# Seven products for one more k pair, and a new order of VectorE's work, in the down stages of a fused fp32 block

## What is computed

```
z = rmsnorm(h, norm2_w) @ mlp_w1          # 2048 -> 8192
h = h + jnp.square(jax.nn.relu(z)) @ mlp_w2   # 8192 -> 2048
h = rmsnorm(h, final_norm_w)
```

## Time and profile before

| | before |
|---|---|
| median of three runs | 2046.81 us |
| the profiled execution | 2047.38 us, span 2045.6 us |
| TensorE matmul busy | 2024.0 us, 99% |
| VectorE busy | 1449.1 us, 71% |
| ScalarE busy | 1268.6 us, 62% |
| first down stage that is done in pairs of chunks | 1422.13 to 1511.33 us |

### The profile page before, as it was taken

One profiled execution on the slowest core, in us unless ns is written; L12 is line 12 of the kernel. 1 busy time (PEld: TensorE's weight loads), 2 busy tenths in 40 slices (PEclk: granted clock), 3 DMA queues, 4 the chain that ended last, 5 costly groups with the idle time before them and its releaser, 6 DMA issues.

```text
span 2045.6 us, 25754 instructions
## 1 busy us (share of the span) xinstructions
PE 2024.0 (99%) x9847; PEld 1705.5 (83%) x9847; DVE 1449.1 (71%) x1930; ACT 1268.6 (62%) x1884; POOL 6.1 (0%) x12
## 2 busy tenths in 40 slices
PE   9999999999999999999999999999999999999998
PEld 8888888888898888888889988888788778878886
DVE  6666566757877777658966567976876876786664
ACT  7666666646566787546566455577448646744754
POOL 0000000000000000000000000000000000000000
PEclk9999999999999999999999999999999999999999
DMA  7766555565656545565655456665565656656664
GB/s 261 211 189 197 170 156 157 182 198 169 208 167 189 166 143 164 187 193 182 195 156 163 136 151 198 189 198 184 182 207 185 202 178 194 187 185 198 209 208 147
DMA packets 198879, 375.48 MB, mean 184 GB/s; under 512 B 13875, under 2 KB 48917, under 8 KB 198230
## 3 DMA queue, kind: packets, MB, share of 16 engines
q1 hardware_dynamic: 198758, 373.85, 59.1%
HBM read 371.71 MB, written 2.10 MB: 183 GB/s over the span
## 4 chain that ended last, share of the span: by engine, by line
PE 91%; DVE 6%; ACT 1%; issue 1%; DMA 1%; SPq 0%; ACTq 0%; DVEq 0%
PE acc L589 23%; PE acc L591 23%; PE acc L590 23%; PE acc L995 2%; PE acc L997 2%; PE acc L996 2%; PE acc L1091 2%; PE acc L1094 2%; PE acc L1093 2%; DVE wlo L1868 2%; PE acc L840 1%; PE tp L601 1%; DVE quad_lo L1896 1%; PE acc L818 1%; PE tp L840 1%
## 5 line engine op out<-in xcount | busy, mean ns | idle before, releaser
L1868 DVE TENSOR_TENSOR wlo<-raw,whi 128x1024 fp32r<-128x1024 f32 x618 | 748.4, 1221 | 383.2 <-ACT whi L1250 380.1
L1250 ACT ACTIVATE whi<-raw 128x1024 fp32r<-128x1024 f32 x618 | 649.8, 1058 | 481.4 <-PE acc L591 356.0
L589 PE MATMUL acc<-whi,both 128*128 128x512 f32 (+1 forms) x592 | 226.7, 383 | 1.0 <-DVE wlo L1873 1.0
L591 PE MATMUL acc<-whi,both 128*128 128x512 f32 (+1 forms) x592 | 224.6, 379 | 0.0
L590 PE MATMUL acc<-wlo,both 128*128 128x512 f32 (+1 forms) x592 | 224.5, 379 | 0.0
L589 PE MATMUL acc<-whi,aT 128*128 128x512 f32 x508 | 200.1, 394 | 0.0
L591 PE MATMUL acc<-whi,bT 128*128 128x512 f32 x512 | 199.2, 389 | 0.0
L590 PE MATMUL acc<-wlo,bT 128*128 128x512 f32 x512 | 199.2, 389 | 0.0
L589 PE MATMUL acc<-whi,bT 128*128 128x512 f32 x512 | 199.2, 389 | 0.0
L591 PE MATMUL acc<-whi,aT 128*128 128x512 f32 x508 | 198.1, 390 | 0.0
L590 PE MATMUL acc<-wlo,aT 128*128 128x512 f32 x508 | 197.8, 389 | 0.0
(11 more groups left out here) (457 smaller groups left out, 3593.8 us busy)
## 6 DMA issues: line engine op xcount, KB each, us to landing
raw<-in_mlp_w SPq DMA_DIRECT2D x256, 512.0 KB, 4.2
raw<-in_w_in_a SPq DMA_DIRECT2D x128, 512.0 KB, 3.9
raw<-in_w_ple_gate SPq DMA_DIRECT2D x64, 512.0 KB, 4.1
raw<-in_w_in SPq DMA_DIRECT2D x64, 512.0 KB, 3.9
raw<-in_w_in_b SPq DMA_DIRECT2D x40, 512.0 KB, 4.1
raw<-in_w_out_a SPq DMA_DIRECT2D x32, 512.0 KB, 4.0
raw<-in_w_out_b SPq DMA_DIRECT2D x32, 512.0 KB, 4.3
raw<-in_w_out SPq DMA_DIRECT2D x32, 512.0 KB, 4.7
```

Of the source, the lines that this page charges most:

```text
L589: pe.matmul(o, hi[:, kt, tok], whi[:, slot, wc], start=start, stop=False)
L591: mm = pe.matmul(o, lo[:, kt, tok], whi[:, slot, wc], start=False, stop=stop)
L1250: act.activation(whi[:, u % RING, 0:n], raw[:, u % RING, 0:n], ACT.Copy).then_inc(hi_done, 1)
L1868: dve.tensor_tensor(wlo[:, u % RING, 0:n], raw[:, u % RING, 0:n], whi[:, u % RING, 0:n].bitcast(F32), ALU.subtract).then_inc(lo_done, 1)
```

## The change

The pair of chunks j = 0 does k pair 1 by seven products too. VectorE makes the sums of a quad one step earlier, right behind the splitting of the unit before it and ahead of that step's hooks. The twelve matmuls of the last k pair but one come one unit later, behind the first three matmuls of the next such pair. In the down stage `lo_moved` goes from step 3 to step 8. The additions to x go to steps 11 and 12 of j = 1 (and 5 and 6 of the next up stage), as functions of their own; the sums themselves stay at steps 0 to 2 of j = 1, and go to 2 to 4 of the up stage. The buffer `shared` becomes three: `second`, and `first` twice.

```diff
-FAST = ((3, 5), (1, 3, 5))
+FAST = ((1, 3, 5), (1, 3, 5))
...
-        shared = sb("shared", [P, 4, CH], F32, tab_at)
+        second = sb("second", [P, 2, CH], F32, tab_at)
+        first = [sb(f"first{i}", [P, 2, CH], F32, (r3 + 4 * KB, tab_at + 4 * KB)[i]) for i in range(2)]
...
                 if b == PAIRED:
                     sp.wait_ge(sem("zs_lo"), PAIRED * len(SUMMED))
+                    sp.wait_ge(sem("pair_x"), 4 * PAIRED)
...
                 def sums_products(uu):
 
-                    g = sums_due(s.u0 + j * s.units + uu, 3)
-                    if g is None:
+                    late = uu - 4 >= 0 and (uu - 4) // 2 == FAST[j][-2]
+                    kt = uu - (3 if late else 2)
+                    g = sums_due(s.u0 + j * s.units + uu, 4 if late else 3)
+                    if g is None or not late and kt // 2 == FAST[j][-2]:
                         return
-                    kt = uu - 2
...
             def first_product_out(n, u):
 
                 act.wait_ge(unit_used, u + 1)
-                if n:
-                    act.wait_ge(sem("pair_x"), 2 * n)
-                act.activation(shared[:, 0, :], tp[0][:, :], ACT.Copy).then_inc(sem("p1_out"), 1)
+                if n >= 2:
+                    act.wait_ge(sem("pair_x"), 2 * (n - 1))
+                act.activation(first[n % 2][:, 0, :], tp[0][:, :], ACT.Copy).then_inc(sem("p1_out"), 1)
...
                     if f and f[1] == 0:
-                        quad_summed(u, f[0])
                         dve.wait_ge(hi_done, u + 1)
...
                         quad_split(sums_due(u, 2))
+                    if sums_due(u, -1) is not None:
+                        quad_summed(u + 1, sums_due(u, -1))
...
                 if q < PAIRED:
+                    if c == QT - 1:
+                        return join(turned, {8: halves[first + 1]})
...
+            def last_sum(n):
                 dve.wait_ge(sem("pair_sums"), 4 * n + 3)
+                dve.tensor_tensor(second[:, 1, :], xb[0][:, :], second[:, 0, :], ALU.subtract).then_inc(sem("pair_sums"), 1)
+
+            def tokens_added(n, t):
+                cols, sums = slice(n % 2 * UNIT, (n % 2 + 1) * UNIT), (first[n % 2], second)[t]
+                dve.wait_ge(sem("pair_sums"), 4 * (n + 1))
                 dve.wait_ge(sem("down_d"), 4 * (n + 1))
...
+            def shared_hooks(n, at, later):
+                return {at: [lambda: product_sums(n)], at + 1: [lambda: more_sums(n)], at + 2: [lambda: last_sum(n)],
+                        later: [lambda: tokens_added(n, 0)], later + 1: [lambda: tokens_added(n, 1)]}
...
-                        hooks = shared_hooks(2 * q - 1, 3) if q else join({q - 1: [lambda q=q: blocks_turned("x5", 3, q)] for q in (2, 3)},
+                        hooks = shared_hooks(2 * q - 1, 2, 5) if q else join({q - 1: [lambda q=q: blocks_turned("x5", 3, q)] for q in (2, 3)},
...
-                    along(s, j, join(shared_hooks(2 * q, 0) if j else z_lo(q, 3),
+                    along(s, j, join(shared_hooks(2 * q, 0, 11) if j else z_lo(q, 3),
```

More of the change, by code:

```diff
@@ L2606, in product_sums @@
                 dve.wait_ge(sem("p1_out"), n + 1)
+                if n:
+                    dve.wait_ge(sem("pair_x"), 2 * n)
                 dve.wait_ge(sem("quad_used"), n // 2 * (len(FAST[0]) + len(FAST[1])) + len(FAST[0]) + n % 2 * len(FAST[1]))
-                dve.tensor_tensor(shared[:, 3, :], shared[:, 0, :], tp[1][:, :], ALU.add).then_inc(sem("pair_sums"), 1)
+                dve.tensor_tensor(second[:, 1, :], first[n % 2][:, 0, :], tp[1][:, :], ALU.add).then_inc(sem("pair_sums"), 1)
@@ L2610, in more_sums @@
             def more_sums(n):
                 dve.wait_ge(sem("pair_sums"), 4 * n + 1)
[L2612 to L2616, removed]
+                dve.tensor_tensor(second[:, 0, :], second[:, 1, :], xb[1][:, :], ALU.add).then_inc(sem("pair_sums"), 1)
@@ L2617, in first_tokens @@
+                dve.tensor_tensor(first[n % 2][:, 1, :], xb[0][:, :], second[:, 1, :], ALU.subtract).then_inc(sem("pair_sums"), 1)
+            def last_sum(n):
                 dve.wait_ge(sem("pair_sums"), 4 * n + 3)
+                dve.tensor_tensor(second[:, 1, :], xb[0][:, :], second[:, 0, :], ALU.subtract).then_inc(sem("pair_sums"), 1)
+            def tokens_added(n, t):
+                cols, sums = slice(n % 2 * UNIT, (n % 2 + 1) * UNIT), (first[n % 2], second)[t]
+                dve.wait_ge(sem("pair_sums"), 4 * (n + 1))
@@ L2618, in first_tokens @@
                 dve.wait_ge(sem("down_d"), 4 * (n + 1))
[L2619 to L2625, removed]
@@ L2627, in shared_hooks @@
-            def shared_hooks(n, at):
-                return {at: [lambda: product_sums(n)], at + 1: [lambda: more_sums(n)], at + 2: [lambda: first_tokens(n)], at + 3: [lambda: last_tokens(n)]}
+                dve.tensor_tensor(x[:, t, cols], x[:, t, cols], sums[:, :, :].rearrange("p i n -> p (i n)"), ALU.add).then_inc(sem("pair_x"), 1)
+            def shared_hooks(n, at, later):
+                return {at: [lambda: product_sums(n)], at + 1: [lambda: more_sums(n)], at + 2: [lambda: last_sum(n)],
+                        later: [lambda: tokens_added(n, 0)], later + 1: [lambda: tokens_added(n, 1)]}
```

## The result

| | before | after |
|---|---|---|
| median | 2046.46 us (5 runs, 2046.13 to 2047.01) | 2056.72 us (5 runs, 2056.48 to 2057.34) |
| span of the profiled execution | 2045.6 us | 2054.9 us |

The ratio is 1.0049, with a 95% interval of 1.0038 to 1.0061: the changed kernel is slower by 10.3 us. The forecast was 2056.3 us.

What follows compares the result with a forecast made beforehand. TensorE, 99% busy, bounds the kernel, and VectorE's order and length of work set its pauses. Per down stage 6.53 + 2.90 - 5.56 - 0.68 = +3.19 us; three stages, +9.5, on 2046.81 give 2056.3 us, range 2051 to 2062.

Steps and rivals of the forecast that it cites:

- The three saved matmuls a stage: In each j = 0 of a down stage, seven products for k pair 1 take away 3 matmuls, 0.68 us a stage.
- The sums of k pair 1: On VectorE in j = 0: 2.60 us of added sums, done by about 1422.2 and hidden before the flips at 1424.67.
- Unit 5 of j = 0: TensorE pauses 2.96 us there: VectorE does the quad's low part and turned blocks first, finishing unit 5 at 1435.87.
- The other pauses of j = 0: TensorE pauses at unit 4 (0.49 us), unit 7 (1.32), unit 9 (0.74) and unit 10 (0.32).
- J = 1: Pauses of 0.43 (acc[1]), 1.73 (unit 5) and 0.32 us (extra banks' fourth sum); with restarts 2.90 against 3.57 us.
- The sum: Each down stage 6.53 + 2.90 - 5.56 - 0.68 = +3.19 us; three stages +9.5 us.
- The fourth: Rival: k pair 1 left as it was or its wait never met, so only the order acts; 2047.6 us, chance 0.02.
- The first: Rival: faster, VectorE finishing unit 5 of j = 0 by 1432.9 rather than 1435.9; 2034 us, chance 0.08.
- the second: Rival: no change, since pauses in j = 0 overlap as in the lower bound; 2046 us, chance 0.12.
- The third: Rival: the clock falls to 1.2 GHz behind the long pauses, +8.2 us in all; 2064.5 us, chance 0.04.
- I kept the clock full through pauses of 3 us: TensorE's granted clock, full in all 40 slices through pauses up to 1.5 us, was assumed full through 3 us.
- my own two signs that the prediction is wrong: First matmul of j = 0 to that of j = 1 under 45 us, or the clock leaving its full level.

## Why the prediction was right

**The three saved matmuls a stage** came as counted: 9838 against 9847.

**The sums of k pair 1** are hidden ahead of the flips as forecast. They started at 1418.61 after a wait of 0.46 us for a load, and VectorE still idled 0.67 us before the flips.

**Unit 5 of j = 0**, the largest term, was put at a pause of 2.96 us: 3.06, 3.06 and 3.04 measured. That it comes from the quad's low part and the blocks ahead of it is shown by three runs: it stays in the old order, 2.5 us more work there lengthens it by 2.5, and with the blocks behind unit 5 it is 1.71. The last also shows what the prediction did not say: without the blocks ScalarE sets the end.

**The other pauses of j = 0** were put at 0.49, 1.32, 0.74 and 0.32 us; 0.58, 1.42, 0.72 and 0.33 were measured in the first stage. From its first matmul to that of j = 1 I had 48.0 us, and it was 48.27.

**J = 1**: 0.43, 1.73 and 0.32 forecast, 0.42, 1.71 and 0.42 measured; 44.4 us forecast, 44.42 measured. The pauses at units 7 and 9 went, and their return with the additions shows why. The second stage has 44.66.

**The sum** was +3.19 us a stage; the stages grew by 3.49, 3.77 and 3.55. Most of the rest are the 0.3 us of j = 0. The nearness of the totals, 2056.3 and 2056.7, is in part luck: the forecast added 9.5 us to a median of 2046.81 from three runs, the five runs of the result table have 2046.46, and the difference of the medians is 10.3 and that of the stages 10.8.

**The rivals.** The fourth was out (k pair 1 is done by seven products), and the run without it gave 2048.9 where I had worked out 2047.6. The first, VectorE in time for unit 5, did not occur, nor did the second. The third came half true: **I kept the clock full through pauses of 3 us, and that was wrong**, though it moved the time by nothing I could measure. A clock that leaves its full level was one of my own two signs that the prediction is wrong, and it came. The sum held all the same, because of a term that it did not have. The granted clock in three stretches of 5 us behind the pause of unit 5, one per stage of the changed kernel (the column after the engines' busy times):

```profile
1434.00:1439.00 5.00, 4.45 (x19) 3.68 (x20) 4.83 (x9) 0.06 (x1) 0.00 (x0) 1.00 0.30 108
1614.00:1619.00 5.00, 4.71 (x14) 3.77 (x15) 4.83 (x9) 0.32 (x1) 0.00 (x0) 0.66 0.31 108
1794.00:1799.00 5.00, 4.74 (x14) 3.74 (x15) 4.83 (x9) 0.35 (x1) 0.00 (x0) 0.66 0.29 108
```

In TensorE's timeline of the second stage the distance of matmuls is 0.43 us at first, the lower level of 1.2 GHz, and comes back to 0.23 after 3 us:

```profile
1614.29 0.79 PE L1093 MATMUL acc<-whi,both 128*128 128x512 f32 x1 [2.90 <-DVE wlo L1870]
1614.88 0.63 PE L1095 MATMUL acc<-wlo,both 128*128 128x512 f32 x1
1615.30 0.63 PE L1096 MATMUL acc<-whi,both 128*128 128x512 f32 x1
...
1617.01 0.62 PE L1093 MATMUL acc<-whi,both 128*128 128x512 f32 x1
1617.44 0.43 PE L1095 MATMUL acc<-wlo,both 128*128 128x512 f32 x1
1617.70 0.40 PE L1096 MATMUL acc<-whi,both 128*128 128x512 f32 x1
1617.94 0.39 PE L1093 MATMUL acc<-whi,both 128*128 128x512 f32 x1
```

I had priced such a fall at 2.72 us a stage. It cost nothing because the next wait, for unit 7, ends at a time that VectorE and ScalarE set: in the second stage the slow matmuls took the place of the 1.42 us that TensorE waited there in the first. J = 0 lasts 48.27, 48.28 and 48.27 us with none, six and seven of them at the slow distance. I had not foreseen this, so that the time came out right in spite of the clock is luck. By the rule of the Trainium skill (TensorE: Matmul & The Clock Gate, section HAM oscillation), that long waits for operands drop the clock to half, the trace agrees as to the clock; the time of the third rival, 2064.5 us, was not seen here.

## What to carry to other kernels

In an engine that is 99% busy, a saving of 0.7 us of its work can make a stretch 2.9 us longer (j = 0 with k pair 1 alone), if the engine that feeds it must do 4.3 us more in a fixed order, 2.2 us of it just ahead of a deadline. Lay out the feeding engine's queue instruction by instruction from the rows, in the new order, before counting what the busy engine saves. A work item whose result is wanted late (here the additions to x) belongs where the feeding engine waits anyway, and one that another engine waits for belongs early. When work is moved ahead on one engine, look at what the other engine does with its result: the turned blocks held up ScalarE, which held up the next unit.

## What was not expected of the hardware

In these profiles the granted clock fell within or just behind 14 of the 15 pauses of TensorE that had 2.9 us or more by the bracket. It fell at none of the shorter ones, of which the longest were 1.6 us in the down stages and 2.2 us once, near the start of the run with the sums back in place. The slow matmuls were 5 to 12 in a stage, at 0.43 us each. What they cost ranged from nothing, where a pause followed, to about 0.4 us a stage, by the estimate above.

A late unit makes a late load. In the run with the nine matmuls and the sums back in place, unit 7's low part was done at 1442.3. The load of unit 11 waits for it, and the sums that need this load began at 1447.40, 5.1 us later, where the median of this weight's loads is 4.2 us. With a ring of four units, a delay can come back four units on, and three on where the sums of a quad need two units at once: pauses of 0.9 to 1.7 us at unit 10 in these two runs, where 0.7 was expected from VectorE's queue.
